# Two blocks in one program: the first two down panels of a chunk issued together, attention factors issued behind the scores, and the state-space input table computed on VectorE in pieces

## The reference

```python
def swiglu(x, w_gu, w_down):                       # four times: ffn0 to ffn3, D_FF = 2816
    g, u = jnp.split(x @ w_gu, 2, axis=-1)
    return (jax.nn.silu(g) * u) @ w_down

# first layer's attention (12 heads), second layer's with compressed, selected and window branches
p = masked_softmax(s, mask); o = jnp.einsum('bhqk,bhkd->bqhd', p, v)

# state space, second block: 48 groups, 64 states each way, 16 channels per group
lam_bar = jnp.exp(lam * step)
b_bar = ((lam_bar - 1.0) / lam)[..., None] * lax.complex(b_re, b_im)
bu = lax.complex(einsum('btgh,gph->btgp', u, b_bar.real), einsum('btgh,gph->btgp', u, b_bar.imag))
_, s = lax.associative_scan(_linear_recurrence, (a, bu), axis=1)
```

## Time and profile before

| | |
|---|---|
| runs shown | 2679.3, 2680.72, 2687.15 us; median 2680.72 |
| the profiled execution | 2677.05 us |
| its span, from first to last instruction | 2675.2 us |
| mean granted TensorE clock | 0.974 of full speed |
| TensorE products busy | 2537.1 us, 95% of the span |
| VectorE busy | 1439.4 us, 54% |
| ScalarE busy | 950.6 us, 36% |
| GpSimd busy | 1041.6 us, 39% |
| moved by DMA | 291.93 MB |

### The profile page before, as it was taken

The page is one execution under the profiler, slowest core; times in us unless marked ns, Lnnn a source line. Parts: engine busy times, 40 slices in busy tenths (PEclk is TensorE's granted clock), DMA queues, the critical chain, the costliest instruction groups (busy, mean ns, idle before and its releaser), DMA issues.

```text
span 2675.2 us, 34403 instructions
## 1 busy us (share of the span) xinstructions
PE 2537.1 (95%) x12622; PEld 2029.8 (76%) x12622; DVE 1439.4 (54%) x2049; ACT 950.6 (36%) x1483; POOL 1041.6 (39%) x698
## 2 busy tenths in 40 slices
PE   7999999898999999999999999889999998988998
PEld 6877887556778887788878777678888876776786
DVE  5545456564655645454644668473333364894453
ACT  3223224463422223332222478453222243353222
POOL 1988874102758942233632412164022054020400
PEclk8999999999999999999999999899999998999999
DMA  7345445311434455244442321135333326433231
GB/s 185 95 120 144 129 117 135 90 28 40 126 113 130 149 134 127 74 146 118 144 140 84 91 71 37 51 97 168 102 118 107 91 82 171 138 127 107 79 95 63
DMA packets 438834, 291.93 MB, mean 109 GB/s; under 512 B 34339, under 2 KB 420186, under 8 KB 435258
## 3 DMA queue, kind: packets, MB, share of 16 engines
q1 hardware_dynamic: 421770, 212.38, 28.3%
q0 software_dynamic: 16944, 77.93, 9.6%
HBM read 272.50 MB, written 20.92 MB: 110 GB/s over the span
## 4 chain that ended last, share of the span: by engine, by line
PE 74%; DVE 9%; POOL 6%; ACT 5%; issue 3%; DMA 2%; SPq 1%; DVEq 0%; ACTq 0%; POOLq 0%
PE ps L759 36%; PE ps L764 18%; PE ps L786 4%; PE ps L770 3%; POOL NS L2828 1%; POOL NS L2827 1%; POOL SW L2830 1%; DVE wl L2066 1%; PE ps L941 1%; ACT wh L1539 1%; PE ps L956 1%; DMA raw<-in_ffn_w_gu 1%; PE ps L1106 1%; DVE PR L2331 1%; PE ps L1072 1%
## 5 line engine op out<-in xcount | busy, mean ns | idle before, releaser
L2066 DVE TENSOR_TENSOR wl<-raw,wh 128x1024 fp32r<-128x1024 f32 x376 | 616.8, 1641 | 958.9 <-ACT wh L1539 955.7
L1539 ACT ACTIVATE wh<-raw 128x1024 fp32r<-128x1024 f32 x385 | 408.4, 1061 | 1377.0 <-PE ps L764 1183.2
L759 PE MATMUL ps<-XH,wh 128*128 128x512 f32 x1848 | 725.5, 393 | 3.5 <-ACT wh L1539 3.5
L759 PE MATMUL ps<-XL,wh 128*128 128x512 f32 x1848 | 720.2, 390 | 0.0
L764 PE MATMUL ps<-XH,wl 128*128 128x512 f32 x1848 | 457.1, 389 | 0.0
L759 PEld LDWEIGHTS ps<-XH,wh 128*128 128x128 f32 x1848 | 347.6, 188 | 80.5 <-ACT wh L1539 4.3
L759 PEld LDWEIGHTS ps<-XL,wh 128*128 128x128 f32 x1848 | 347.5, 188 | 73.8 <-issue 2.2
L764 PEld LDWEIGHTS ps<-XH,wl 128*128 128x128 f32 x1848 | 346.8, 188 | 72.3 <-issue 0.4
L759 PE MATMUL ps<-HH,wh 128*128 128x512 f32 x552 | 219.6, 398 | 0.0
L759 PE MATMUL ps<-HL,wh 128*128 128x512 f32 x552 | 217.9, 395 | 0.0
L2936 POOL TENSOR_TENSOR NS<-AW,CS 128x2048 f32<-128x2048 f32 x32 | 116.7, 3646 | 233.3 <-PE ps L1020 223.4
(11 more groups left out here) (494 smaller groups left out, 3946.6 us busy)
## 6 DMA issues: line engine op xcount, KB each, us to landing
raw<-in_ffn_w_gu SPq DMA_DIRECT2D x176, 512.0 KB, 3.8
raw<-in_ffn_w_down SPq DMA_DIRECT2D x64, 512.0 KB, 4.1
AW<-in_ada_w POOLq DMA_DIRECT2D x24, 1024.0 KB, 6.9
raw<-in_ffn_w_down SPq DMA_DIRECT2D x32, 384.0 KB, 3.4
BS<-s_b POOLq DMA_DIRECT2D x12, 1024.0 KB, 6.4
raw<-in_odd_w_in SPq DMA_DIRECT2D x24, 512.0 KB, 3.7
raw<-in_even_w_in SPq DMA_DIRECT2D x22, 512.0 KB, 4.2
s_w<-SW POOLq DMA_DIRECT2D x12, 512.0 KB, 6.9
```

The source lines that it names most:

```text
L759: pe.matmul(ps[:, p % 4, 0:n], wh[:, p % 2, k * P:(k + 1) * P], x[:, k, 0:n], start=k == 0 and x is hi, stop=False)
L1539: act.activation(wh[:, p % 2, :], raw[:, p % 4, :], ACT.Copy).then_inc(w_hi, 1)
L2066: dve.tensor_tensor(wl[:, p % 2, :], raw[:, p % 4, :], wh[:, p % 2, :].bitcast(F32), ALU.subtract).then_inc(w_lo, 1)
```

## The change

Five things change.

1. TensorE issues the first two down panels of each chunk together (`down_pair`): for k from 0 to the last but one, three products of the first panel each; then the second panel's products with `wh` for the same k; then it waits for the last k, does it for both, and the second panel's products with `wl` come last. The other six down panels are unrolled; they stood in a loop in the first two chunks.
2. In the first attention TensorE issues the second scores of a pair ahead of the factors.
3. In the second attention it does the same for the second factors of a pair but the last, and ScalarE does its exponentials ahead of the copy of those factors.
4. In ffn0, GpSimd's product for `BK` is left out. VectorE makes it, six pieces for a tile (`bk_ops`), placed by hand between its evictions, with ffn0's loops unrolled (`ffn0`, `up`, `residual`). `bt_dve` counts the last piece too.
5. TensorE's fill waits for the last piece (`bt_dve`) ahead of the transposes, and for GpSimd's strip (`bk_ready`) only behind them.

```diff
+            def down_pair(stage, off, nf, need):
+                p = BASE[stage] + off
+                pe.wait_ge(w_lo, p + 1)
+                pe.wait_ge(taken[p % 4], p // 4)
...
+                for k in range(nf - 1):
+                    pe.wait_ge(*need(k))
+                    for w, x in ((wh, HH), (wl, HH), (wh, HL)):
+                        product(0, k, w, x)
+                pe.wait_ge(w_hi, p + 2)
+                pe.wait_ge(taken[(p + 1) % 4], (p + 1) // 4)
+                for k in range(nf - 1):
+                    for x in (HH, HL):
+                        product(1, k, wh, x)
+                pe.wait_ge(*need(nf - 1))
+                for w, x in ((wh, HH), (wl, HH), (wh, HL)):
+                    mm = product(0, nf - 1, w, x)
+                mm.then_inc(pe_panel, 1)
+                for x in (HH, HL):
+                    product(1, nf - 1, wh, x)
+                pe.wait_ge(w_lo, p + 2)
+                for k in range(nf):
+                    mm = product(1, k, wl, HH)
+                mm.then_inc(pe_panel, 1)
...
                     need = lambda k: (h_ready, f0 + k + 3)
+                    down_pair(stage, off, nf, need)
                     if c < 2:
-                        with pe.Fori(0, KD // 4) as i:
-                            for j in range(4):
-                                panel(stage, off + j, i, HH, HL, nf, need=need if j == 0 else None)
+                        for j in range(2, KD):
+                            panel(stage, off + j, 0, HH, HL, nf)
                     else:
-                        for j in range(KD):
+                        shift(stage, 0)
+                        shift(stage, 1)
+                        for j in range(2, KD):
...
             def s5_fill(t):
-                pe.wait_ge(bk_ready, t + 1)
+                pe.wait_ge(bt_dve, 3 * t + 1)
                 wait(pe, z_out, 4 * t)
                 wait(pe, bt_act, 2 * t)
-                wait(pe, bt_dve, 2 * t)
...
                 pe.wait_ge(bt_act, 2 * t + 1)
+                pe.wait_ge(bk_ready, t + 1)
...
                 probs_t(2 * i + 1, 1)
+                mla_scores(2 * i + 3, 1)
                 mla_factors(i, 2 * i + 4)
-                mla_scores(2 * i + 3, 1)
...
                 else:
+                    nsa_scores(u + 5, 1, 1 - q)
                     nsa_factors(j, 1)
-                    nsa_scores(u + 5, 1, 1 - q)
                     nsa_pv(j, 1)
...
                 probs_out(u + 3, 1)
-                factors_out(PAIR["nsa"] + 2 * j + 1, 6 if last else 3)
                 if last:
+                    factors_out(PAIR["nsa"] + 2 * j + 1, 6)
                     mem_exp(u + 5, 5, 1)
                 else:
                     softmax_exp(u + 5, 1)
+                    factors_out(PAIR["nsa"] + 2 * j + 1)
...
+            def up(stage, off, f0, f):
+                p = BASE[stage] + off + 2 * f
+                u = p + 1
+                rest(p + 2)
+                rest(p + 3)
...
+            def residual(stage, at, j, scale, q=None):
+                p = BASE[stage] + at
+                rest(p + 2)
+                dve.wait_ge(pe_panel, p + 1)
...
+            def bk_ops(t, parts):
...
+                for part in parts:
+                    e, a = divmod(part, 3)
+                    if part == 0:
+                        if t == 0:
+                            dve.wait_ge(f_ready, 2)
+                        wait(dve, s5_t, 4 * t)
+                    if part == 1:
+                        wait(dve, s5_out, 32 * t)
+                    if part > 0:
+                        dve.wait_ge(s5_dve, s5_steps[0])
+                    if a == 0:
+                        ins = dve.tensor_tensor(dst[e], bb[0], pb_[e], ALU.mult)
+                    elif a == 1:
+                        ins = dve.tensor_tensor(tmp, bb[1], pb_[1 - e], ALU.mult)
+                    else:
+                        ins = dve.tensor_tensor(dst[e], dst[e], tmp, (ALU.subtract, ALU.add)[e])
...
+            def ffn0():
+                stage, off, f0 = "ffn0", 0, 0
+                for f in range(8):
+                    up(stage, off, f0, f)
+                    if f >= 5:
+                        bk_ops(0, (2 * f - 10, 2 * f - 9))
+                s5_fill(0)
+                for j in range(KD):
+                    residual(stage, 16 + j, j, 2 * ALPHA)
+                    if j >= 2:
+                        bk_ops(1, (j - 2,))
+                s5_fill(1)
+                for f in range(4):
+                    up(stage, 24, 8, f)
+                    bk_ops(2, ((0,), (1, 2), (3, 4), (5,))[f])
+                s5_fill(2)
+                for f in range(4, 8):
+                    up(stage, 24, 8, f)
+                    bk_ops(3, ((0,), (1, 2), (3, 4), (5,))[f - 4])
+                s5_fill(3)
+                for j in range(KD):
+                    residual(stage, 40 + j, j, 1.0, 16 + j)
+                    if j >= 2:
+                        bk_ops(4, (j - 2,))
+                s5_fill(4)
+                for f in range(6):
+                    up(stage, 48, 16, f)
+                    bk_ops(5, (f,))
+                s5_fill(5)
...
             def tile(t):
-                wait(pool, s5_t, 4 * t)
-                inputs = [BK[:, r].rearrange("p g (h t) -> p g t h", t=L) for r in range(2)]
-                product(over_time(BB), over_channels(PB), [(ALL, inputs)], [P, GT, L, S5H])
```

More of the change, by code:

```diff
@@ L804, in pair, with product @@
                 mm.then_inc(pe_panel, 1)
+            def down_pair(stage, off, nf, need):
+                p = BASE[stage] + off
+                pe.wait_ge(w_lo, p + 1)
+                pe.wait_ge(taken[p % 4], p // 4)
+                def product(e, k, w, x):
+                    return pe.matmul(ps[:, (p + e) % 4, :], w[:, (p + e) % 2, k * P:(k + 1) * P], x[:, k, :],
+                                     start=k == 0 and w is wh and x is HH, stop=k == nf - 1 and w is (wh, wl)[e] and x is (HL, HH)[e])
+                for k in range(nf - 1):
[17 more added lines that the diff above has]
+                mm.then_inc(pe_panel, 1)
             def panels(stage, count, need, hi=XH, lo=XL, nk=8, after=None):
@@ L841, in ffn @@
                     need = lambda k: (h_ready, f0 + k + 3)
+                    down_pair(stage, off, nf, need)
                     if c < 2:
-                        with pe.Fori(0, KD // 4) as i:
-                            for j in range(4):
-                                panel(stage, off + j, i, HH, HL, nf, need=need if j == 0 else None)
-                    else:
-                        for j in range(KD):
-                            panel(stage, off + j, 0, HH, HL, nf, need=need if j == 0 else None,
-                                  within=(lambda: running_sum(stage)) if j == KD - 1 else None)
+                        for j in range(2, KD):
+                            panel(stage, off + j, 0, HH, HL, nf)
+                    else:
+                        shift(stage, 0)
+                        shift(stage, 1)
+                        for j in range(2, KD):
+                            panel(stage, off + j, 0, HH, HL, nf, within=(lambda: running_sum(stage)) if j == KD - 1 else None)
                             shift(stage, j)
@@ new lines, in residual @@
+            def residual(stage, at, j, scale, q=None):
+                p = BASE[stage] + at
+                rest(p + 2)
+                dve.wait_ge(pe_panel, p + 1)
+                if q is not None:
+                    dve.wait_ge(*taken_at(stage, q))
+                dve.scalar_tensor_tensor(XT[:, j, :], XT[:, j, :], scale, ps[:, p % 4, :], ALU.mult, ALU.add).then_inc(taken[p % 4], 1)
+            def bk_ops(t, parts):
+                gs = slice(t * GT, (t + 1) * GT)
+                bb = [BB[:, r, gs, :].rearrange("p g (h o) -> p g h o", o=1).broadcast_to([P, GT, S5H, L]) for r in range(2)]
+                pb_ = [PB[:, r, gs, :].rearrange("p g (o t) -> p g o t", o=1).broadcast_to([P, GT, S5H, L]) for r in range(2)]
+                dst = [BK[:, r].rearrange("p g (h t) -> p g h t", t=L) for r in range(2)]
+                tmp = BT[:, 0].rearrange("p g (h t) -> p g h t", t=L)
+                for part in parts:
[14 more added lines that the diff above has]
+                        ins = dve.tensor_tensor(dst[e], dst[e], tmp, (ALU.subtract, ALU.add)[e])
+                    if part < 5:
+                        ins.then_inc(s5_dve, 1)
+                        s5_steps[0] += 1
+                    else:
+                        ins.then_inc(bt_dve, 1)
@@ new lines, in ffn0 @@
+            def ffn0():
[27 more added lines that the diff above has]
+                s5_fill(5)
+                for j in range(KD):
+                    down(stage, 60 + j, j, 1.0, lambda d: taken_at(stage, 40 + d))
@@ L2389, in _ @@
             s5_parameters()
-            ffn("ffn0", s5_fill)
+            ffn0()
             norm("ffn0", 4e-5)
```

19 lines of the change are left out of this document (13 added, 6 removed).

## The result

The changed kernel takes **2704.0 us** (median of 8, 2694.84 to 2713.15) where the kernel before takes 2681.12 (8 runs): a ratio of **1.009**, 95% interval 1.0067 to 1.0114. It is 0.9% slower. Measured again at the end of the study it was 1.0105 (1.0073 to 1.0138), 2705.91 against 2679.96. By the ratios that is 24 us and 28 us (the medians lie 22.9 and 26.0 apart), where the sum said 15.8.

What follows compares the result with a forecast made beforehand. TensorE, busy 95% of the span, bounds the kernel, so only its idle stretches and clock count. 26.2 + 8.5 - 12.8 - 1.5 - 4.6 = plus 15.8 us: 2692.9 profiled, 2696.5 against the median; range 2687 to 2708.

Steps and rivals of the forecast that it cites:

- a term held at zero: Clock in code the change doesn't touch, behind the last feed-forward stage: the sum gave it no time.
- The fills' waits, plus 26.2: ffn0's six fills: TensorE's transposes wait for VectorE's last table piece, behind the last eviction; 26.2 us more in all.
- The clock behind them, plus 8.5: Behind the five new fill stalls TensorE's clock halves, 1.7 us lost each, 8.5 in all; ends 0 and 17.
- Down panels woven, minus 12.8: All four feed-forward stages: five waits for the last low half go, 9.4 us, and 3.4 of half clock behind two.
- The named risk: Woven down panels: VectorE's low half for the third panel may come late, 0 to 1 us each; taken as 0.
- First attention, minus 1.5: First attention: the projection's wait for ScalarE's copy replaces the factors' wait in four pairs; 1.5 us less, ends 0 and 4.9.
- Second attention, minus 4.6: Second attention: the waits for gated sums go in five pairs; 4.6 us less, ends 2.5 and 5.1.
- the 0.5 us subtracted because VectorE would slip: Second attention: VectorE, wanted earlier, slips some 0.7 us, partly absorbed by idle time; 4.6 taken from 5.1 us held.
- The first, the table ready in time: ffn0's fills: GpSimd's waits and their lost clock go, nothing comes; 26.7 us less in all, 2654; chance 0.04.
- The second, that the clock stays up: ffn0's fills: no half clock behind the new stalls; plus 7.3 in all, 2688.0; chance 0.16.
- The third, that pieces meet GpSimd at a fill: At three fills one final VectorE operation takes 4.51 us, not 1.23, beside GpSimd; plus 9.8, 2706; chance 0.12.
- the agreement on the ratio of the two engines: Table work: GpSimd's six operations took 15.0 us, VectorE's would take 7.4, agreeing with the skill's about twice as slow.

Runs made afterwards that it cites:

- early_pieces: The changed kernel with the same 36 VectorE pieces issued one eviction sooner, the last ahead of the last low half: 2662.76 us, 0.9934 of the kernel before.
- late_pieces: The changed kernel with two pieces, not one, behind the last eviction ahead of fills 1 to 5: 2710.64 us, one run.
- warm_fills: The changed kernel with unused TensorE products put ahead of each fill's wait for the last piece: 2690.74 us, 1.0028 of the kernel before.
- after_again: The changed kernel, unchanged, profiled and timed a second time: 2705.91 us, 1.0105 of the kernel before.
- before_again: The kernel before, unchanged, profiled a second time: 2671.96 us, one run.
- scores_only: The kernel before with only the moved calls of the two attentions: 2673.13 us, 0.9956 of the kernel before.
- table_only: The kernel before with only the input table moved to VectorE, panels unwoven and attentions in their old order: 2723.61 us, 1.0161 of the kernel before.
- weave_only: The kernel before with only the woven first two down panels (`down_pair`): 2671.46 us, 0.9961 of the kernel before.
- no_table: The changed kernel with the table left on GpSimd, keeping woven panels and both attention orders: 2663.82 us, 0.9928 of the kernel before.

## Why the prediction was right, and where its sum was off

The forecast, slower by the table's place, came out: 2704.0 in a range of 2687 to 2708, forecast 2696.5. The waits and the clock behind them came as the prediction had them. That the sum of 15.8 lies under the 24 and 28 has another cause, a term held at zero, which is the last step here. By its steps:

- **The fills' waits, plus 26.2**: right. 31.4 less 6.1 is 25.3; the six were given as 6.8, 4.3, 5.6, 5.6, 4.3 and 5.7 and measured 6.72, 4.14, 5.46, 5.46, 4.14 and 5.47. That the place decides, and not the amount of work, is shown from both sides by early_pieces (none) and late_pieces (1.26 more for each piece more).
- **The clock behind them, plus 8.5**: right in kind and a little under-sized: warm_fills gives 11.6 from fill 0 on, of which fill 0's own 1.7 were not the step's, so 10 for the five new stalls, and 12 by after_again. The step took one stretch of 3.41 us at half clock for each new stall. Three of the five were 6.83 long in after, as at fill 0 (27.3 us in place of 17, of which 6.3 lie in the stalls themselves), and all five in after_again.
- **Left out of the sum**: two low halves of the third block come 0.83 us late behind two pieces, 1.7 us (two of the three L764 waits above). I had looked only at the last block ahead of the fill.
- With these three the stage accounts for itself: 25.3, 10 to 12 and 1.7 make 37 to 39; its end lies 37 to 41 us later after than before (464.1 and 466.1 against 425.5 and 427.1).
- **Down panels woven, minus 12.8**: right, at its upper end. In the panel of ffn1 whose last low half ends at 820.93, k=7 is called for at 822.13, 8.1 us after the start (8.0 was worked out) and 1.2 after the low half:

```profile
814.02 0.47 PE L813 MATMUL ps<-HH,wh 128*128 128x512 f32 x1
...
822.13 0.39 PE L813 MATMUL ps<-HH,wh 128*128 128x512 f32 x1
```

```profile
819.43 1.50 DVE L2200 TENSOR_TENSOR HL<-HF,HH 128x512 f32 x1
```

  Stage ffn1 takes 384.8 and 385.6 us where it took 390.4 to 393.4 (before_again; scores_only and table_only), ffn2 428.9 where it took 433.0. (In the first profile of before ffn1 took 396.1, with one wait of 2.4 us for ScalarE's cast in it.) The 3 us between 390.4 and 393.4 is the clock term: half clock for 3.4 us of the stage in before_again and for 10 to 14 in the other two. So the gain is 10 to 14 us by stretches and 10 by the clocked runs. The named risk, a low half late for the third panel, is there once for 0.71 us.
- **First attention, minus 1.5**: right. From first to last product with the values, 67.75 became 66.44, twice each: minus 1.3. The wait did change places, from the factors to the projection, at a length of 0.79 where the earlier trace rows had 0.82.
- **Second attention, minus 4.6**: under-sized, and outside its ends of 2.5 and 5.1. From first to last, 112.1 us (before_again, weave_only, table_only; 113.9 in the first profile of before, with 3.4 us at half clock) became 105.85: **minus 6.3**. The step that failed is the 0.5 us subtracted because VectorE would slip, which reached TensorE nowhere, and the size of the wait: the idle column understates it. A pair went from 20.23 us to 18.86, which is 1.37 for a wait printed as 1.07.
- **The total.** The parts come to 37 to 39 less 1.3, less 6.3, less 10 to 14, so 15 to 21 us. Measured are 24 (interval 18 to 31) and 28 (20 to 37). The intervals reach down to that, but the spans differ by more, 26 and 35, and the stretch of unchanged code shows where: 6 and 14 us of it, at the lower clock. Why the full clock is granted less often there isn't settled. As far as single profiles tell it needs neither the table (no_table has 524.8 us in this stretch, weave_only 522.8) nor the weave (table_only has 528.3); scores_only has 517.5, near before. But one part of the stretch is longer in every kernel that differs from before, scores_only too: the same 131 products in and around the norm in it take 24.7 and 25.8 us in the two profiles of before, and 32.3 to 33.7 in all eleven others, 30.6 us or more of that at half clock where before had some 10. What in the changed kernels brings this about is not shown. My forecast held this term at zero.

**The rivals.** The first, the table ready in time, did not happen, and early_pieces, which makes it so by placing the pieces otherwise, gained 0.7% where 26.7 us, 1.0%, was worked out for it. The second, that the clock stays up, did not happen; warm_fills is what it would have been: 0.28% over before, 7.5 us, where plus 7.3 was given. The third, that pieces meet GpSimd at a fill, did not happen at any of the six: the last piece took 1.22 or 1.23 each time. Elsewhere it did:

```profile
L2139 DVE TENSOR_TENSOR BK<-BB,PB x12: 1212/2032/3424, 130.7 to 427.5; 128x1024 f32<-128x1024 f32 x12
L2143 DVE TENSOR_TENSOR BK<-BK,BT x12: 1218/1220/3308, 140.3 to 449.2; 128x1024 f32<-128x1024 f32 x12
```

(Shortest, median and longest in ns.) The Trainium skill (SBUF — State Buffer, Who interferes with whom) says that a VectorE instruction with two inputs in SBUF and one of GpSimd that reads SBUF exclude each other. All but one of the 36 agree: 15 lie beside GpSimd's work and took 2.36 to 3.42 us, 20 where GpSimd was idle took 1.21 to 1.23 (the one left, at 134.1 us, took 1.23 beside it). **A reading of mine that doesn't hold** is the agreement on the ratio of the two engines. With 1.9 us a piece over the stage VectorE gained 62.3 us of busy time and GpSimd lost 72.4 over the span, a ratio of 1.2, not two (instruction by instruction, the 36 took 92.9 us on GpSimd before and 69.5 on VectorE after, 1.3): six times the 1.23 us of an undisturbed low half was no price for a piece beside GpSimd. The Trainium skill (GPSIMD Engine Reference, Engine selection) has two-input elementwise work about twice as slow on GpSimd; no run here shows that over the 36. And the table on the faster engine, well placed, bought nothing that the ratios show over the slower one that had the time: 0.9934 and 0.9913 against 0.9928.

## What to carry to other kernels

When work moves to another engine, its price is less than its place: put the last piece ahead of an instruction that waits for the consumer's own progress, in the idle slot in front of it, never behind it, for then the consumer waits for its own end, a hand-off through other engines and the piece. Look for the slot by the idle entries of the receiving engine, one piece to a slot. And count behind every new stall of TensorE the products at half clock: here some 10 us on top of 25.3.

## What the runs showed that I had not expected

- The granted clock costs time where nothing was changed. One norm's stretch behind the last feed-forward stage, in after_again; and the stretch around the fall in the same norm in before, which holds fewer products:

```profile
2210.22:2244.35 34.13, 28.25 (x133) 18.66 (x133) 19.23 (x29) 16.62 (x25) 17.73 (x15) 0.50 0.17 62
```

```profile
2204.00:2232.00 28.00, 21.88 (x89) 15.86 (x89) 20.82 (x23) 12.84 (x15) 16.11 (x12) 0.82 0.34 109
```

  34.13 us at 1.2 GHz without a break, where before fell for 10.24 us. In the whole tail 36 and 42 us at half clock before became 59 and 82.
- The idle column of TensorE is no measure of what a removed wait gives back: 1.07 printed, 1.37 gained per pair.
- Two profiles of one kernel lie 5.0 us (before) and 4.0 us (after) apart, with 138 and 124, and 189 and 205 us at half clock. A difference of a few us between two profiles has to be read by stretches and their clock, and by the timed runs.
